# Layer-norm sums ahead of most first-half output rows, embedding pieces behind the router, and an fp32 token gather that comes out turned

## What is computed

```python
proj = h @ w_in                                    # six groups of 512 columns
o = gated linear recurrence over 32-frame chunks   # group A, 512 wide
c = jax.nn.silu(_layernorm(causal_conv(u), conv_ln_g, conv_ln_b))   # group B, 512 wide
x = x + jnp.concatenate([o, c], axis=-1) @ w_out
x = x + _moe(_rmsnorm(x, norm_ffn), ...)           # top 4 of 32 experts, clamped SwiGLU, every expert's weights read
x = x + jax.nn.sigmoid(_rmsnorm(x, norm_ple) @ w_ple_gate) * (pe @ w_ple)
y = _rmsnorm(x, norm_final)
```

## Time and profile before

| | |
|---|---|
| runs | 1218.29, 1217.98, 1221.67 us |
| profiled execution, its own time | 1219.33 us |
| its span, first to last instruction | 1217.5 us |
| mean granted TensorE clock | 0.983 of full speed |
| TensorE matmul busy | 1125.7 us (92%) |
| VectorE, ScalarE, GpSimd busy | 387.3, 232.8, 39.5 us |
| HBM read | 428.53 MB |
| HBM rate in the expert loop (slices of the page) | 427 to 430 GB/s |
| chain that ended last, by engine | PE 68%, DMA 26%, DVE 3%, ACT 1%, issue 1% |

### The profile page before, as it was taken

The page is one execution under the profiler, slowest core; times in us unless marked ns, Lnnn a source line. Parts: engine busy times, 40 slices in busy tenths (PEclk is TensorE's granted clock), DMA queues, the critical chain, the costliest instruction groups (busy, mean ns, idle before and its releaser), DMA issues.

```text
span 1217.5 us, 14744 instructions
## 1 busy us (share of the span) xinstructions
PE 1125.7 (92%) x5871; PEld 462.0 (38%) x5871; DVE 387.3 (32%) x838; ACT 232.8 (19%) x370; POOL 39.5 (3%) x23
## 2 busy tenths in 40 slices
PE   5999989899999999999989898989898989899986
PEld 4775655433333333333323232323232323233333
DVE  5568975621313212121212121212130303031234
ACT  3531114412020101111111111111202020211124
POOL 3340000100000000000000000000000000000000
PEclk9998999699999999999999999999999999999998
DMA  9913121699999999999999999999999999999911
GB/s 288 365 37 139 43 104 42 239 386 430 428 427 428 430 428 428 428 430 427 429 428 429 428 428 428 430 428 429 428 429 428 429 428 430 428 428 428 427 44 39
DMA packets 44057, 430.73 MB, mean 354 GB/s; under 512 B 4885, under 2 KB 8933, under 8 KB 19359
## 3 DMA queue, kind: packets, MB, share of 16 engines
q1 hardware_dynamic: 39016, 425.42, 83.7%
q10 hardware_dynamic: 5015, 4.95, 1.2%
HBM read 428.53 MB, written 1.83 MB: 353 GB/s over the span
## 4 chain that ended last, share of the span: by engine, by line
PE 68%; DMA 26%; DVE 3%; ACT 1%; issue 1%; SPq 0%; ACTq 0%; DVEq 0%
PE ps L779 34%; DMA ring<-in_w_gate_up 24%; PE ps L480 7%; PE ps L470 5%; PE ps L739 5%; PE ps L704 4%; PE ps L798 4%; DMA ring<-in_w_down 2%; PE ps L714 2%; PE ps L788 1%; PE ps L504 1%; PE ps L747 1%; PE ps L544 1%; PE ps L562 1%; PE ps L706 1%
## 5 line engine op out<-in xcount | busy, mean ns | idle before, releaser
L779 PE MATMUL ps<-ring,arena 128*64 128x512 f32 x2048 | 466.7, 598 | 19.4 <-DMA ring<-in_w_gate_up 19.4
L798 PE MATMUL ps<-ring,arena 128*64 128x512 f32 x1024 | 232.3, 598 | 30.8 <-DMA ring<-in_w_down 13.6
L779 PEld LDWEIGHTS ps<-ring,arena 128*64 128x64 f32 x2048 | 136.5, 137 | 296.0 <-issue 255.7
L798 PEld LDWEIGHTS ps<-ring,arena 128*64 128x64 f32 x1024 | 68.5, 137 | 171.2 <-issue 113.6
L1694 DVE TENSOR_TENSOR acc<-ps,acc 128x512 f32<-128x512 f32 x64 | 44.2, 691 | 212.8 <-PE ps L739 212.8
L1580 DVE CAST arena<-cst 96x128 bf16 (+1 forms) x17 | 3.8, 222 | 273.0 <-PE ps L779 273.0
L1104 ACT COPY arena<-ps 128x512 f32<-128x512 f32 x32 | 18.7, 586 | 328.9 <-PE ps L788 328.9
L480 PE MATMUL ps<-ring,arena 128*128 128x512 f32 x140 | 64.3, 615 | 1.1 <-DVE arena L1472 1.1
L470 PE MATMUL ps<-arena,ring 128*128 128x288 f32 x256 | 64.2, 410 | 0.7 <-DVE arena L1249 0.7
L1599 DVE TENSOR_TENSOR arena<-ps,par 128x256 f32<-128x256 f32 x68 | 25.5, 417 | 121.5 <-PE ps L779 118.4
L739 PE MATMUL ps<-arena 128*128 128x512 f32 x128 | 63.5, 619 | 0.0
(11 more groups left out here) (267 smaller groups left out, 799.9 us busy)
## 6 DMA issues: line engine op xcount, KB each, us to landing
ring<-in_w_gate_up SPq DMA_DIRECT2D x128, 2048.0 KB, 24.4
ring<-in_w_down SPq DMA_DIRECT2D x64, 2048.0 KB, 23.1
ring<-in_w_in SPq DMA_DIRECT2D x5, 2048.0 KB, 20.5
ring<-in_w_out SPq DMA_DIRECT2D x2, 2048.0 KB, 15.8
ring<-in_w_in SPq DMA_DIRECT2D x2, 1024.0 KB, 11.9
arena<-in_w_ple_gate ACTq DMA_DIRECT2D x2, 768.0 KB, 5.6
arena<-in_w_ple_gate ACTq DMA_DIRECT2D x1, 1280.0 KB, 10.2
acc<-in_x_prompt SPq DMA_DIRECT2D x2, 512.0 KB, 4.5
```

The costliest lines, as they stand in the source:

```text
L779: t = mm(ps[h * 64:h * 64 + 64, G + 2 * e + g, :], xT[:, 2 * kk + c, e * 64:e * 64 + 64], w[:, c, lo:lo + 512], start=False, stop=(kk == 3 ...
L798: t = mm(ps[n * 64:n * 64 + 64, PP + e, :], hidT[:, 4 * e + c, half * 64:half * 64 + 64], w[:, c, n * 512:(n + 1) * 512], start=(half == 0 ...
```

## The change

Three edits in one.

1. On TensorE the mean matmuls come after only half of `out_first(0)`, and the variance matmuls before `turn_outputs(2)`, `out_first(1)` and `out_first(2)`.
2. All six `per_layer` pieces move behind the router: 0, 1, 3, 2 right behind it, 4 and 5 behind the position sums; they get other PSUM banks, and ScalarE copies all of them, behind the last root and ahead of the router's exponentials.
3. The three-way bf16 split, its two scratch tiles, the copy of the gathered rows and the transposes go. `xn2` stays fp32 in SBUF and is the stationary operand (every second column of it, 128 of them), a fp32 one-hot `sel` of 128 columns is the moving one: 8 chunks x 3 blocks = 24 fp32 matmuls, whose result is already turned. SyncE's conditions for the units stay as they are.

```diff
-            def out_first(b):
+            def out_first(b, halves=range(2)):
...
-                for n in range(2):
+                for n in halves:
                     row_block(mixT, wout[n], b, X_BANK[b][n], range(4), DC - 1)
 
-            out_first(0)
+            out_first(0, [0])
...
-            turn_outputs(2)
-            out_first(1)
+            out_first(0, [1])
...
             t.then_inc(S["var_mm"], 1)
+            turn_outputs(2)
+            out_first(1)
             out_first(2)
 
-            pe.wait_ge(full[2], 32)
-            pe.wait_ge(S["cvar"], 1)
...
-            for i in range(4):
-                if i >= 2:
-                    pe.wait_ge(S["pl_ready"][i - 2], 1)
-                per_layer(i)
...
             router(1)
             router(2)
-            per_layer(4)
+            pe.wait_ge(full[2], 32)
+            for i in PL_ORDER[:4]:
+                per_layer(i)
...
             t.then_inc(S["pos_mm"], 1)
+            per_layer(4)
+            pe.wait_ge(S["pl_ready"][3], 1)
             per_layer(5)
...
                 pe.wait_ge(S["sel_ready"], j + 1)
-                for n in range(2):
-                    cols = slice(n * 512, (n + 1) * 512)
-                    for b in range(2):
-                        for k in range(3):
-                            mm(ps[:, PP + n, :], selb[:, b, :], xsb[:, b, k, cols],
-                               start=(b == 0 and k == 0), stop=False)
-                    mm(ps[:, PP + n, :], selb[0:96, 2, :], xssb[0:96, cols],
-                       start=False, stop=True).then_inc(S["gath_mm"], 1)
-
-            def turn_tokens(j):
-                for n in range(2):
-                    pe.wait_ge(S["gath_ev"], j * 2 + (n + 1))
-                    for c in range(4 * n, 4 * n + 4):
-                        lo = 256 * (c // 2) + c % 2
-                        t = tr(ps[:, PP + n, (c % 4) * P:(c % 4 + 1) * P], gath[:, lo:lo + 255:2], ident)
-                    t.then_inc(S["xt3_mm"], 1)
+                for c in range(DC):
+                    lo = 256 * (c // 2) + c % 2
+                    for b in range(NB):
+                        t = mm(ps[:, PP + c // 4, (c % 4) * P:(c % 4 + 1) * P],
+                               xn2[0:ROWS[b], b, lo:lo + 255:2], sel[0:ROWS[b], b, :],
+                               start=(b == 0), stop=(b == NB - 1), skip_group_check=True)
+                    if c % 4 == 3:
+                        t.then_inc(S["gath_mm"], 1)
...
                 gate_up(3)
-                turn_tokens(j + 1)
                 gate_up(4)
```

More of the change, by code:

```diff
@@ L146, in program @@
         xs = sb("xs", 2 * 3 * D // 2)
-        xs_s = sb("xs_s", D // 2)
+        sam = sb("sam", D // 2)
         bias = sb("bias", D)
@@ L214, in program @@
         csq = blocks(U_flat[:, 0:H * T], H)
-        Ss = xs_s[:, 0:W]
+        Ss = sam[:, 0:W]
+        sel = blocks(sam[:, 0:NB * P])
         ubs = KdT_flat[:, 0:H * T]
@@ L227, in program @@
         croot = xs[:, 2016:2016 + T]
-        xn2 = blocks(arena[:, A_CONV + 2 * D:A_CONV + 5 * D])
-        junk2 = arena[:, A_CONV + 5 * D:A_CONV + 6 * D]
+        xn2 = blocks(xs[:, 0:NB * D])
+        junk2 = arena[:, A_CONV:A_CONV + D]
         wr = arena[:, A_QD:A_QD + DC * E]
@@ L244, in ex @@
             return arena[:, at2[0] - n:at2[0]]
-        gath = ex(D)
         xT = blocks(ex(D), DC)
+        selg = blocks(ex(NB * P))
+        oneh = ex(P // 2).bitcast(BF16)
+        ex(64)
+        gw = ex(T)
+        ex(D - 64 - T - NB * P - P // 2)
         gbuf, sgm, ubuf = ex(D), ex(D), ex(D)
@@ L251, in program @@
         ybuf = ex(D)
[L252 to L255, removed]
         eye = cst[:, C_EYE:C_EYE + E + 2]
@@ L316, in program @@
         PG_BANK = (4, 5, 6, 7, 0, 1)
-        PL_BANK = (3, 4, 3, 4, 7, 6)
+        PL_BANK = (1, 2, 5, 7, 6, 7)
+        PL_ORDER = (0, 1, 3, 2, 4, 5)
         X_BANK = ((1, 2), (5, 6), (7, 0))
@@ L670, in _ @@
                     row_block(mixT, wout[n], b, X_BANK[b][n], ks, DC - 1).then_inc(S["out_mm"], 1)
-                if b == 1:
-                    for i in (2, 3):
-                        pe.wait_ge(S["pl_ready"][i], 1)
                 if b:
@@ L699, in gather @@
                 pe.wait_ge(S["sel_ready"], j + 1)
-                for n in range(2):
-                    cols = slice(n * 512, (n + 1) * 512)
-                    for b in range(2):
-                        for k in range(3):
-                            mm(ps[:, PP + n, :], selb[:, b, :], xsb[:, b, k, cols],
-                               start=(b == 0 and k == 0), stop=False)
-                    mm(ps[:, PP + n, :], selb[0:96, 2, :], xssb[0:96, cols],
-                       start=False, stop=True).then_inc(S["gath_mm"], 1)
-            def turn_tokens(j):
-                for n in range(2):
-                    pe.wait_ge(S["gath_ev"], j * 2 + (n + 1))
-                    for c in range(4 * n, 4 * n + 4):
-                        lo = 256 * (c // 2) + c % 2
-                        t = tr(ps[:, PP + n, (c % 4) * P:(c % 4 + 1) * P], gath[:, lo:lo + 255:2], ident)
-                    t.then_inc(S["xt3_mm"], 1)
-            pe.wait_ge(S["xs_l"], NB)
+                for c in range(DC):
[6 more added lines that the diff above has]
+                        t.then_inc(S["gath_mm"], 1)
+            pe.wait_ge(S["xn2_ready"], NB)
+            pe.wait_ge(S["pl_ready"][2], 1)
             gather(0)
-            turn_tokens(0)
             pe.wait_ge(S["gat_ready"], 1)
-            pe.wait_ge(S["pl_ready"][4], 1)
-            pe.wait_ge(S["pl_ready"][5], 1)
+            for i in (0, 1, 4, 5):
+                pe.wait_ge(S["pl_ready"][i], 1)
             for b in range(NB):
@@ L1003, in _ @@
             fn(croot, croot, ACT.Sqrt).then_inc(S["csqrt"], 1)
-            act.wait_ge(S["gated"], NB)
             def per_layer(i):
                 n, b = divmod(i, NB)
-                act.wait_ge(S["pl_mm"], i + 1)
+                act.wait_ge(S["pl_mm"], PL_ORDER.index(i) + 1)
                 rows_out(lambda rows, cols, x: copy(ple3[rows, b, cols], x), PL_BANK[i], b, n
                          ).then_inc(S["pl_ready"][i], 1)
-            per_layer(0)
-            per_layer(1)
             for cc in range(H):
@@ L1021, in _ @@
             act.dma_start(ybuf[0:E, :], a["b_down"][0]).then_inc(S["bd_in"], 16)
[L1024 to L1043, removed]
             def tokens_hi(b):
@@ L1057, in _ @@
             root(1, 0)
-            high(0)
-            middle(0)
             tokens_hi(0)
             square_of(1)
-            low(0)
             square_of(2)
@@ L1067, in _ @@
             root(1, 2)
[L1068 to L1075, removed]
+            act.wait_ge(S["gated"], NB)
+            for i in PL_ORDER[:4]:
+                per_layer(i)
             act.wait_ge(S["top_ready"], 1)
@@ L1080, in _ @@
                    accum_out=wsum[:, b:b + 1]).then_inc(S["wexp"], 1)
[L1082 to L1085, removed]
             per_layer(4)
@@ L1091, in _ @@
             gate_chunks(gate0, 0, FREE, 0)
-            copy_gathered(0)
             act.wait_ge(S["gT_mm"], 1)
@@ L1097, in step @@
             def step(j):
-                copy_gathered(j + 1)
                 for n in range(2):
@@ L1188, in _ @@
                 nc.gpsimd.tensor_tensor(lk, kf, lev, ALU.mult).then_inc(S["lev_k"], 1)
[L1190 to L1196, removed]
         @block.vector
@@ L1461, in _ @@
                                 ALU.mult, ALU.add).then_inc(S["cn_ready"], 1)
[L1463 to L1469, removed]
             for cc in range(H):
@@ L1520, in _ @@
             normalise(2)
-            remainder(1, 0)
             zero_rest(lg[:, 2, :])
@@ L1575, in select @@
                 dve.wait_ge(S["sel_cur"], j + 1)
-                V.tensor_tensor(selb.rearrange("p b (e s) -> p (b e) s", e=2), iota_s, per_slot(cur),
+                V.tensor_tensor(sel.rearrange("p b (e s) -> p (b e) s", e=2), iota_s, per_slot(cur),
                                 ALU.is_equal).then_inc(S["sel_ready"], 1)
@@ L1597, in tokens_out @@
                 for n in range(2):
-                    dve.wait_ge(S["xt3_mm"], j * 2 + (n + 1))
+                    dve.wait_ge(S["gath_mm"], j * 2 + (n + 1))
                     ins = V.tensor_tensor(xT[:, 4 * n:4 * n + 4, slots],
```

18 lines of the change are left out of this document (2 added, 16 removed).

## The result

The changed kernel takes 1240.09 us (median of four runs, 1238.03 to 1244.57); the kernel before, in the runs measured beside it, 1219.98. The ratio is 1.0164, with a 95% interval of 1.0121 to 1.0207: **slower by 1.6%**, where 1214.4 us and faster was forecast.

A forecast was written before the change was run, and what follows sets the result against it. Expert loop bound by the weight stream, 58.7 us a step against TensorE's 55.0. Front -6.6, step 0 +2.3, last step +0.4 sum to -3.9 us: 1214.4 us against the median of 1218.29, range 1211.0 to 1219.5.

The forecast's parts named there:

- Output rows earlier: Front part: the convolution half of the output rows starts at 187.2 instead of 193.1, 5.9 us earlier.
- Residual and router: Front part: without the bf16 subtractions holding VectorE, the router ends near 211.8 instead of 219.0, 7.2 us earlier.
- The clock: Behind the router: clock falls, then four dense per_layer pieces bring it back, taking 8 us instead of 6.0.
- that rival: Low clock reaches the gather before the loop: gather up to 11 us, total 1216.5 to 1219.5, chance 0.15.
- The front as a sum: All up to the loop: first matmul at 230.5 against 237.05, 6.6 us earlier, with a gather of 6.0.
- The size of G: G is the fp32 gather's time: 24 matmuls, 48 weight loads at 0.122 us plus 0.1, so 6.0 us.
- Inside the loop: Expert loop: a step needs 56.7 us of TensorE, still under the memory's 58.7, so mostly no cost.
- a rival that got 0.06: Weight loads not hidden: gather 10.0 us, TensorE step 60.7 us, about 1262 us, slower; chance 0.06.
- 6.6 to 7.2: Gather dearer but still hidden, fp32 passes and stride adding up: +1.8 to +3.6 us, 1216 to 1218; chance 0.14.
- the three counts of G: Gather time counts three times in the total: in the front, step 0 and the last step.
- The two small edges of the loop: Longer gather delays the weight stream in step 0 by 2.3 us and ends the last step 0.4 late.

The follow-up runs named there:

- e1: The change, with the gather's third block multiplied with all 128 rows (zeros in the one-hot) instead of 32: 1212.57 us, ratio to before 0.9928.
- e5: The change, with the 32-row matmuls taken two at a time, so four switches to 32 rows and back per gather: 1216.18 us, ratio 0.9962.
- e3: The change, with xn2 stored permuted so the stationary operand is contiguous, the 32-row block kept: 1230.12 us in one run.
- e6: The change, with all 128 rows in the third block and a contiguous stationary operand: 1211.45 us, ratio 0.9927.
- e8: e1 with the layer-norm sums in the order of before and the per_layer pieces still behind the router: 1218.86 us, ratio 0.9979.
- e9: The change, with 64 rows instead of 32 in the third block's matmuls: 1241.99 us in one run.
- e2: The change, with a bank's 32-row matmuls behind its eight 128-row ones, start flag only on the bank's first matmul: 1214.51 us, ratio 0.9948.
- e10: The change, with 96 rows instead of 32 in the third block's matmuls: 1210.3 us in one run.

## Why the prediction was wrong

- **Output rows earlier: right.** The second half was to start 22.0 us behind `out_first(0)` (187.2 - 165.2); it starts 22.1 behind it in the change (191.65 - 169.56), in e1 too. The idle stretch ahead of the variance was to be 1.5 us and is 0.7 to 1.65.
- **Residual and router: right.** The router's wait on VectorE fell from 1.17 us to 0.40.
- **The clock: right in kind, the size a little high.** It fell and came back among the `per_layer` pieces, as the windows of the change show (clock is the third number from the end):

```profile
214.00:216.00 2.00, 2.00 (x18) 1.94 (x18) 0.17 (x3) 0.00 (x0) 0.00 (x0) 0.50 1.00 426
...
218.00:220.00 2.00, 2.00 (x4) 0.76 (x3) 1.83 (x7) 0.10 (x1) 0.00 (x0) 0.69 0.99 426
220.00:222.00 2.00, 2.00 (x6) 0.95 (x5) 0.12 (x2) 0.92 (x2) 0.00 (x0) 1.00 0.00 0
```

  The pieces took 6.7 us for the full ones and 0.6 for the small one, instead of 8. The gather ran at the high level (clock 1.00 in every window from 220 to 240; in every kernel the first one, ahead of the loop, took within 0.06 us of those in the loop); that rival did not come.
- **The front as a sum.** Forecast -6.6 us with a gather of 6.0. e1, whose gather is 5.85, has 63.0 us from `out_first(0)` to the loop against 71.9: -8.9. The 2 us more are the pieces (7.1 us instead of 8), the router's own matmuls (3.00 us in e1, where the clock fell only during them, instead of the 4.2 put in and the 4.62 of before) and small waits.
- **The size of G: the step that failed.** "48 x 0.122 + 0.1 = 6.0, which I take, since that row has the same pattern." The pattern of the columns was the same, the pattern of the rows was not: the 24 matmuls go 128, 128, 32 rows. With equal rows the figure holds (5.85 in e1), and with eight changes to 32 rows and back it is 2.9 us more. Neither of the two rows that G was taken from mixes row counts: the loads of the earlier trace rows have 128 rows, and those of the state updates have 32 throughout. The listing of loads by shape, which I had before the prediction, says so in its first column of shapes, and it had the stall as well, in its last column, the idle time ahead of the loads:

```profile
L544 PEld LDWEIGHTS ps<-ple,arena 32*128 32x128 f32 x72 | 8.3, 187 | 4.0 <-issue 3.0 <-DVE arena L1370 1.0
L822 PEld LDWEIGHTS ps<-cst,arena 32*128 32x128 f32 x16 | 2.2, 137 | 2.7 <-issue 2.7
```

  L822 are the three transposes ahead of the `down` units, two of 128 rows and one of 32. Ahead of each of the sixteen 32-row loads PEld stood idle for 0.17 us. One of them in time:

```profile
1144.18 0.20 PEld L822 LDWEIGHTS ps<-cst,arena 128*128 128x128 f32 x2 [0.81 <-issue]
1144.55 0.14 PEld L822 LDWEIGHTS ps<-cst,arena 32*128 32x128 f32 x1 [0.17 <-issue]
```

  The two alike overlap, and the third starts 0.17 us after they have ended: a gap of the same kind, once a step.
- **Inside the loop: the mechanism was right, and it was put into the wrong case.** The edge was set at G = 7.4, and e5 (7.21) and e3 (8.44) lie on its two sides. It belonged to a rival that got 0.06 since it was tied to loads that do not overlap at all (G = 10.0, 1262 us). The cause was another, and between 6.0 and 10.0 the text had only "6.6 to 7.2". An edge behind which each microsecond costs sixteen, 1.4 us above the value taken, deserved a case of its own, whatever would carry G over it. With G = 8.75 the same working gives 16 x (50.7 + 8.75) = 951 us for the loop (950.3 measured) and a front of -3.9 (-4.3): 1218.3 + 26 - 3.9 = 1240. Below the edge the three counts of G (front, step 0, last step) hold roughly: from e1 to e5 the gather grows by 1.36 us and the total by 3.6.
- **The two small edges of the loop** (step 0 and the last step) were put at 2.7 us for G = 6.0; e1's loop is 1.1 us longer than before's. The terms are there, and at half the size or less.
- **The Trainium skill.** Its page TensorE: Matmul & The Clock Gate (Part 3) says in its list of what overlaps that loads overlap running matmuls only where the row group differs. By the windows above it is nearly the reverse here: loads of equal shape overlap, and a load stalls where the rows go from 128 to 32. The text above that list also lets a load go ahead into a background weight buffer, which the prediction left out and which fits the equal loads. The section on LDWEIGHTS in the same page of the Trainium skill says that a 32x128 load takes as long as a 128x128 one; one by one that is so (0.19 and 0.20 us), but it does not price the change from one to the other. The Trainium skill's Advanced Engine Details and Errata (Memory Cachelines) would make every second fp32 free; e6 against e1 shows 0.3 us in 48 loads, 6 ns each: nearly.

What stays open: why a load waits there, beyond that it no longer starts together with the matmul ahead of it. Rows of 32, 64, 96 and 128 were tried next to 128, all from row 0 and all fp32, those of 64 and 96 in one run each; whether a bf16 operand stalls, or a block that starts at another row, was not.

## What to carry to other kernels

Price a run of matmuls from a row with the same sequence of operand shapes, not only the same operand: here a third block padded with zeros to 128 rows, more arithmetic, took a gather from 8.75 to 5.85 us. Where a loop is bound by memory with a few per cent to spare, write down the figure at which the engine becomes the bound, and give a chance to every way across it: here a microsecond of gather cost the loop between one and two below that figure, and one for each step above it. Matmuls moved out of a place may have been filling a wait: without the edit that shortens the wait (e8), most of the gain of the two together (e1) is lost.

## What the runs showed of the hardware

- An fp32 weight load of 32 or 64 rows after one of 128 rows starts 0.31 to 0.32 us after it instead of 0.11 to 0.12, and so does the next one of 128 rows (windows of the change and of e9): 0.19 us more for each change inside a gather (e2, e5, the change, against e1). With 96 rows there is none of it (e10).
- Equal loads of 128 fp32 columns overlap with the matmuls of 128 columns: 24 matmuls in 5.55 us contiguous (e6), 5.85 with every second element (e1), though each of their 48 loads lasts 0.19 to 0.20 us.
- In e8 TensorE's wait of 4.4 us, with the granted clock still at 1.00, was followed by a clock of 0.50, the 1.2 GHz level, and by row blocks that took 15.7 us instead of 14.0.
